# Hybrid decoder step with 32 experts: four rows of each gate-up matrix in one load of 4 MB, the other four in two loads of 2 MB

## What is computed

```python
x = x + (g_a * branch_a + g_b * branch_b) @ w_o           # mixer, from one projection h @ w_in
x = x + moe_ffn(rms_norm(x), ...)
# moe_ffn: 32 experts, the 4 best of a token's logits, their softmax as weights
hgu  = xblk @ w_gu[e] + b_gu[e]                            # 1024 x 2048, float32: 8 MB per expert
gate = minimum(hgu[:, :1024], 7); up = clip(hgu[:, 1024:], -7, 7)
act  = gate * sigmoid(1.702 * gate) * (up + 1)
y    = act @ w_down[e] + b_down[e]                         # 1024 x 1024, float32: 4 MB per expert
```

## Time and profile before

| what | us |
|---|---|
| median of three executions | 1143.05 |
| lowest and highest | 1141.73 and 1143.15 |
| the profiled execution's own time | 1143.05 |
| its span, from the first to the last instruction | 1141.3 |
| PE busy in the span | 1067.8 (94%) |
| mean rate of the DMA engines over the span | 380 GB/s |

### The profile page before, as it was taken

The page is one execution under the profiler, slowest core; times in us unless marked ns, Lnnn a source line. Parts: engine busy times, 40 slices in busy tenths (PEclk is TensorE's granted clock), DMA queues, the critical chain, the costliest instruction groups (busy, mean ns, idle before and its releaser), DMA issues.

```text
span 1141.3 us, 16947 instructions
## 1 busy us (share of the span) xinstructions
PE 1067.8 (94%) x6977; PEld 509.0 (45%) x6977; DVE 414.4 (36%) x716; ACT 173.0 (15%) x295; POOL 2.9 (0%) x12
## 2 busy tenths in 40 slices
PE   2999998699999999999999999999999999999995
PEld 2999964344433333333333434434333333333332
DVE  4366333523333333333333333333333333333344
ACT  4344112211111011011111111111111011001111
POOL 1000000000000000000000000000000000000000
PEclk9899999799999999999999999999999999999998
DMA  9464694799999999999999999999999999999993
GB/s 291 118 185 151 214 397 177 276 430 428 424 431 428 427 431 428 427 430 427 429 388 419 425 427 430 427 429 430 427 429 430 427 428 428 429 428 428 427 424 151
DMA packets 50997, 433.18 MB, mean 380 GB/s; under 512 B 5032, under 2 KB 21952, under 8 KB 25073
## 3 DMA queue, kind: packets, MB, share of 16 engines
q1 hardware_dynamic: 48535, 429.99, 90.9%
q10 hardware_dynamic: 2434, 2.79, 0.8%
HBM read 431.62 MB, written 1.39 MB: 379 GB/s over the span
## 4 chain that ended last, share of the span: by engine, by line
PE 56%; DMA 34%; DVE 4%; issue 3%; ACT 1%; SPq 1%; ACTq 0%; DVEq 0%
DMA down_ring<-in_w_down_dram 20%; PE PS L771 18%; PE PS L797 15%; DMA gu_ring<-in_w_gu_dram 14%; PE PS L627 9%; PE PS L736 3%; PE PS L748 2%; PE PS L679 2%; PE PS L663 1%; PE PS L660 1%; PE PS L749 1%; PE PS L784 1%; PE PS L782 1%; PE PS L811 1%; DVE pick_twice L1114 1%
## 5 line engine op out<-in xcount | busy, mean ns | idle before, releaser
L771 PE MATMUL PS<-gu_ring,XgT 128*64 128x512 f32 x2048 | 471.0, 599 | 9.3 <-DMA gu_ring<-in_w_gu_dram 8.6
L771 PEld LDWEIGHTS PS<-gu_ring,XgT 128*64 128x64 f32 x2048 | 134.3, 136 | 275.4 <-issue 242.3
L797 PE MATMUL PS<-down_ring,actT 128*64 128x512 f32 x992 | 221.7, 596 | 14.0 <-DMA down_ring<-in_w_down_dram 14.0
L1143 DVE TENSOR_TENSOR Y<-PS,Y 128x1024 f32<-128x1024 f32 (+1 forms) x96 | 117.0, 1220 | 267.9 <-PE PS L749 267.9
L1174 DVE SCALAR_TENSOR_TENSOR y_low<-PS,slot_gate,y_high 128x512 fp32r<-128x512 f32 x31 | 23.3, 751 | 310.8 <-ACT y_high L546 310.8
L797 PEld LDWEIGHTS PS<-down_ring,actT 128*64 128x64 f32 x992 | 67.7, 137 | 142.8 <-issue 118.7
L558 ACT ACTIVATE work<-PS 128x512 f32<-128x512 f32 x32 | 19.1, 597 | 471.5 <-PE PS L771 471.5
L627 PE MATMUL PS<-h_high,win_high 128*128 128x264 f32 (+1 forms) x256 | 75.1, 293 | 6.5 <-DVE h_low L930 6.5
L627 PE MATMUL PS<-h_high,win_low 128*128 128x264 f32 (+1 forms) x256 | 74.6, 291 | 0.0
L627 PE MATMUL PS<-h_low,win_high 128*128 128x264 f32 (+1 forms) x256 | 74.5, 291 | 0.0
L736 PE MATMUL PS<-pick,XP 128*128 128x64 bf16 x1792 | 58.6, 194 | 1.0 <-DVE pick L1106 1.0
(11 more groups left out here) (179 smaller groups left out, 659.8 us busy)
## 6 DMA issues: line engine op xcount, KB each, us to landing
gu_ring<-in_w_gu_dram SPq DMA_DIRECT2D x120, 2048.0 KB, 27.0
down_ring<-in_w_down_dram SPq DMA_DIRECT2D x62, 2048.0 KB, 23.1
gu_ring<-in_w_in_dram SPq DMA_DIRECT2D x16, 1024.0 KB, 5.5
gu_ring<-in_w_gu_dram SPq DMA_DIRECT2D x16, 1024.0 KB, 13.1
down_ring<-in_w_o_dram SPq DMA_DIRECT2D x1, 4096.0 KB, 17.4
gu_ring<-in_w_down_dram SPq DMA_DIRECT2D x4, 1024.0 KB, 25.7
gu_ring<-in_w_pool_up_dram SPq DMA_DIRECT2D x1, 2048.0 KB, 7.3
gu_ring<-in_w_conv_out_dram SPq DMA_DIRECT2D x1, 2048.0 KB, 7.5
```

The costliest lines, as they stand in the source:

```text
L771: last = mm(PS[SLOTS * h:SLOTS * h + SLOTS, b, :], XgT[:, k, :], w[:, D * b + HALF * h:D * b + HALF * h + HALF], start=(k == 0), stop=(k = ...
L797: last = mm(PS[SLOTS * h:SLOTS * h + SLOTS, bank, :], acts[:, f % 4, f // 4, :], weights[:, f, HALF * h:HALF * h + HALF], start=(f == 0), ...
L1143: tt(Y[rows, t, :].rearrange("p (h n) -> p h n", h=2), PS[rows, bank:bank + 2, :], Y[rows, t, :].rearrange("p (h n) -> p h n", h=2), ALU.a ...
```

## The change

`GROUPS` names the loads of a matrix by their first row and number of rows. Rows 0 to 3 come in one load of 4 MB, in which partition p takes four neighbouring rows of 512 in memory, 32 KB in one run. Rows 4, 5 and 6, 7 stay loads of 2 MB. Each matrix has three semaphores instead of four; the first stands at 16 times four after the single loads of items 0 and 1, which the wait's value takes in. SyncE waits ahead of the merged load for `gu_used` at 8i - 12, that is four rows of item i-2 instead of two. PE waits ahead of rows 0, 4 and 6. The gather takes its columns with a stride of four elements for rows 0 to 3, and `load_row` fetches its rows from the matching places.

```diff
+GROUPS = ((0, 4), (4, 2), (6, 2))
...
-        gu_landed = [sem(f"gu_landed{s}") for s in range(KT)]
+        gu_landed = [sem(f"gu_landed{s}") for s in range(2 * len(GROUPS))]
...
+        def group(k):
+            return next((g, at, n) for g, (at, n) in enumerate(GROUPS) if at <= k < at + n)
...
             def load_row(e, parity, k):
-                m, r = divmod(k, 2)
+                g, at, n = group(k)
                 sp.dma_start(gu_ring[:, KT * parity + k, :],
-                             w_gu[0, e, 2 * P * m:2 * P * m + 2 * P, :].rearrange("(p r) n -> p r n", r=2)[:, r, :]
-                             ).then_inc(gu_landed[CH * parity + m], 16)
-
-            def load_gu(e, parity, m):
-                src = w_gu[0, bass.ds(e, 1), 2 * P * m:2 * P * m + 2 * P, :].rearrange("a (p r) n -> (a p) (r n)", r=2)
-                sp.dma_start(gu_ring[:, KT * parity + 2 * m:KT * parity + 2 * m + 2, :].rearrange("p s n -> p (s n)"),
-                             src).then_inc(gu_landed[CH * parity + m], 16)
+                             w_gu[0, e, P * at:P * at + P * n, :].rearrange("(p r) n -> p r n", r=n)[:, k - at, :]
+                             ).then_inc(gu_landed[len(GROUPS) * parity + g], 16)
+
+            def load_gu(e, parity, g):
+                at, n = GROUPS[g]
+                src = w_gu[0, bass.ds(e, 1), P * at:P * at + P * n, :].rearrange("a (p r) n -> (a p) (r n)", r=n)
+                sp.dma_start(gu_ring[:, KT * parity + at:KT * parity + at + n, :].rearrange("p s n -> p (s n)"),
+                             src).then_inc(gu_landed[len(GROUPS) * parity + g], 16)
...
             def item_gu(i, e, parity):
-                for m in range(CH):
-                    sp.wait_ge(gu_used, 8 * i + (2 * m - 14))
-                    load_gu(e, parity, m)
+                for g, (at, n) in enumerate(GROUPS):
+                    sp.wait_ge(gu_used, 8 * i + (at + n - 16))
+                    load_gu(e, parity, g)
...
                 for k in range(KT):
-                    m, r = divmod(k, 2)
+                    _, at, width = group(k)
                     for n, (part, t) in enumerate(parts):
                         last = mm(PS[:, 5, SLOTS * k:SLOTS * k + SLOTS],
-                                  XP[:, part, 2 * P * m:2 * P * m + 2 * P].rearrange("t (p r) -> t r p", r=2)[:, r, :],
+                                  XP[:, part, P * at:P * at + P * width].rearrange("t (p r) -> t r p", r=width
+                                                                                   )[:, k - at, :],
...
                 for k in range(KT):
-                    if k % 2 == 0:
-                        pe.wait_ge(gu_landed[CH * u + k // 2], landed)
+                    g, at, width = group(k)
+                    if k == at:
+                        pe.wait_ge(gu_landed[len(GROUPS) * u + g], landed + 16 * (width - 2))
```

## The result

The changed kernel takes 1147.5 us (median of six executions, 1146.34 to 1148.81) against 1142.73 us. The ratio is 1.0045 with a 95% interval of 1.0033 to 1.0056, so 5.1 us slower with an interval of 3.8 to 6.4 (the difference of the two medians is 4.8). A second set of five executions gave 1.0045 again (1.0028 to 1.0062). The forecast was 1145.9 us, +2.8.

A forecast was written before the change was run, and what follows sets the result against it. The DMA stream was taken to bound two long stretches, so the end feels the stream's start, its rate and PE's work after the last awaited load. 1.4 - 2.0 + 3.4 = +2.8 us on 1143.05: 1145.9 us, range 1142.0 to 1149.5.

The forecast's parts named there:

- The bound: In two stretches, about 385 to 620 and 812 to 1003 us, DMA sets the pace; PE waits 1.95 us per item.
- One sign: Second DMA-bound stretch would begin one or two items sooner than 812 us.
- Term 2: Merged loads of items 2 to 28: longer runs save 0.075 us per load, -2.0 us in all.
- Term 3: Item 28, last gate-up wait: rows 0 to 3 become usable together, so PE lags two rows, +3.4 us.
- Term 1: Item 2's first gate-up load is issued at 223.69 instead of 220.26 into an empty queue: +1.4 us, at most 3.4.
- Small things: Gather's stride of four elements: taken as zero, at worst 0.45 us an item, 1.3 us behind the last wait.
- A: Merged loads: long runs bring nothing, cut up or cost by bytes; +4.8, 1147.9 us; chance 0.15.
- B: Not slower: merged loads gain more than the line, break-even 0.18 us per 4 MB; 1142.4 us at 0.2; chance 0.20.
- C: Long runs slower in memory: merged loads at 421 GB/s cost 0.16 us more each, 1152.2 us; chance 0.05.
- D: A fixed cost per queued load goes away, PE's DMA waits vanish, 29.4 us in all: 1113.7 us; chance 0.02.

The follow-up runs named there:

- SyncE's wait alone: Kernel before, with the first gate-up load of every item issued only when four rows are used: 1.0044, +5.0 us; repeated 1.0035, +4.0 us.
- the wait at item 2: Kernel before, with only the first gate-up load of item 2 waiting for four used rows instead of two: 1.0035, +4.0 us.
- the gather's stride: Kernel before, with the gather reading token columns at a stride of four elements for rows 0 to 3, weights in old order: 0.9997.
- the changed kernel with the old gather: Changed kernel, with the gather's old stride of two for all rows, weights in new order: 1.0040, +4.6 us against the kernel before.
- PE's wait alone: Kernel before, with PE waiting for rows 0 to 3 ahead of row 0, loads unchanged: 1.0028, +3.2 us.
- the first repair: Changed kernel, with item 2's rows 0 to 3 in two 2 MB loads, the first issued at two used rows: 1.0019, +2.2 us against the kernel before.
- the kernel with both waits: Kernel before, with first loads issued at four used rows and PE waiting for rows 0 to 3 ahead of row 0: 1.0067, +7.7 us.

## Why the prediction held, and where it was off

Direction and range were right; the forecast size, +2.8, was too small by 2.0 us against the medians and 2.3 against the ratio. By its steps:

**The bound.** There are still two stretches in which the DMA stream sets the pace and PE waits 1.6 to 1.9 us per item. Periods fell from 29.37 to 29.29 us (in the second stretch 29.2 and 29.4 in turn, of which the last two rows below show one), and items without waits took 27.50 us. One sign did not come: the second stretch did not begin an item or two sooner. In both kernels it begins with the same item, whose period is 27.95 us before and 28.97 now. Timeline of the changed kernel's first transposes:

```profile
703.30 0.55 PE L789 MATMUL PS<-ident,pick_twice 128*128 128x128 f32 x3
730.80 0.55 PE L789 MATMUL PS<-ident,pick_twice 128*128 128x128 f32 x3
...
902.56 0.55 PE L789 MATMUL PS<-ident,pick_twice 128*128 128x128 f32 x3
931.95 0.55 PE L789 MATMUL PS<-ident,pick_twice 128*128 128x128 f32 x3
```

**Term 2, the rate: right.** From the issue of the first gate-up load to the landing that PE waits for at item 27 (26 merged loads) the changed kernel takes 973.99 - 224.56 = 749.43 us and, in its second profile, 973.89 - 224.37 = 749.52. The kernel before takes, in its second profile, 970.58 - 219.12 = 751.46. That is 2.0 us, 0.077 per merged load, forecast 0.075. The other profiles agree: 751.3 to 751.6 us in four profiles without merged loads (both runs of SyncE's wait alone, the wait at item 2, the gather's stride) and 749.2 in the changed kernel with the old gather. The first profile of the kernel before has 974.12 - 220.26 = 753.86, as its load stood behind the 1 MB of the single row, 2.45 us. It can be read from single loads too: with the queue full a merged load lands 9.71 to 9.72 us behind the load ahead of it, two loads of 2 MB take 2 x 4.893 = 9.79. By the pages the changed kernel has 42124 DMA packets of 512 bytes or more and the kernel before 45965; the 3841 fewer are the 30 merged loads with 128 packets less each, so the longer runs were not cut up. The straight line through packets of 1 and 16 KB carries to 32 KB.

**Term 3, the lag behind the last wait: right.** It was forecast at +3.4 and measured alone at +3.2 (1.9 to 4.6). The waits went from three of 0.65 us to one per item, as written, and item 28 begins 3.8 us later than before where about 3.5 was expected.

**Term 1, the start of the stream: the mechanism right, the size wrong.** It was put at +1.4, with 3.4 as its most; alone it measured +4.0 (2.5 to 5.5). The step that failed is "the wait for that count now ends at 223.69": it took the time of four used rows, and the distance of the single row in front, from one execution. There item 0 began at full clock, two rows took 3.4 us, and the single row in front was issued 1.2 us before the load. In three further profiles of kernels with the old start (the second of before, PE's wait alone, the gather's stride) item 0 began at half clock and earlier; full clock at that place was seen once more, in the first repair's profile. In the second profile of before the single row, which waits for VectorE and not for PE, left 3.3 us ahead of the load (215.84 and 219.12). Two rows took 5.6 us there, and four took 9.4 in the profile of the wait at item 2 alone. The issue moved by 3.8 us and with nothing left in the queue nearly all of it was lost: the DMA share from 221 to 225 us is 0.94 in the second profile of before, 0.02 in the changed kernel and 0.05 with the wait at item 2 alone. The upper bound of 3.4 fell with the same assumption, since it was the full clock's time for two rows. No kernel with the late issue was profiled with the clock already full at item 0, so whether +1.4 would hold there is not shown. The merged load itself took 12.2 us from issue to landing in the first profile and 13.6 in the second, forecast 12.5.

With the measured 4.0 in place of 1.4 the sum is 4.0 - 2.0 + 3.4 = 5.4 us; measured 5.1, with an interval of 3.8 to 6.4.

**Small things.** The gather's price, taken as nothing with 1.3 us as its bound, is 0.12 us an item and vanishes in the total.

**Rivals.** A, long runs that bring nothing, would have given 1147.9 us, closer to the measured time than the forecast; yet its mechanism is refuted by the landings and periods, and the kernel with both waits speaks against it. A total that fits is no proof of its parts. B, which needs 0.18 us per merged load, and C, which makes them slower, are out with the 0.077. D, the fixed cost of about 2.0 us per load that the Trainium skill ("DMA: Bandwidth & Descriptors", the anatomy of one DMA) fits for loads issued by GpSimd, is not paid between the queued loads of SyncE here: a merger saved 0.08 us. It is seen where the queue is empty, as the cost of a new start: 2 MB took 7.6 us from issue to landing in the profile of the wait at item 2 alone, against 4.9 from landing to landing. (D's sum in the prediction is off by 0.1: 14 x 1.95 + 2 is 29.3.)

## What to carry to other kernels

A merged load is issued when the last of its space is free, and it is useful when the last of it has landed. Where a stream sets the pace, both delays cost nothing in its middle and their full length at its two ends, the first load and the last awaited one. Price the start from more than one execution, or from both levels of the clock: a count of used rows is a time only if PE's clock is known. The rate gain is per packet, so it is worth counting packets before merging: here 27 x 0.08 us stood against two delays of 3 to 4 us.

## What was not expected of the hardware

The granted clock fell to half for some 3 to 4 us at several places where PE was busy, and 24 matmuls then took 7.07 instead of 5.37 us. Windows of the changed kernel (granted clock third from the end):

```profile
850.00:970.00 120.00, 112.71 (x740) 46.13 (x736) 38.08 (x60) 12.27 (x24) 0.00 (x0) 1.00 1.00 429
...
976.00:980.00 4.00, 4.00 (x16) 1.51 (x14) 0.23 (x1) 0.00 (x0) 0.00 (x0) 0.76 1.02 434
1012.00:1016.00 4.00, 4.00 (x12) 1.24 (x14) 1.22 (x1) 0.00 (x0) 0.00 (x0) 0.57 1.01 430
```

Between 790 and 1003 us seven of the eight profiles of kernels with one undivided wait per item showed one to three such falls, the six profiles of kernels with three short waits none. They were largely absorbed by the next DMA wait: behind the fall at 943.46 in the profile of PE's wait alone it is 0.24 us instead of 1.9. Behind the last wait nothing absorbs the 1.7 us of a fall. There most profiles of either kind have one (seven of the eight, five of the six), such as the second profile of the kernel before:

```profile
1004.00:1008.00 4.00, 4.00 (x12) 1.12 (x12) 1.23 (x1) 0.00 (x0) 0.00 (x0) 0.73 1.01 430
```

So they don't explain the difference between the kernels. The first of these observations fits a wait of 1.6 to 1.9 us as a cause: the kernel with PE's wait alone differs from the one before in nothing but the waits. But no run varied the length of a wait step by step, and what sets the falls behind the last wait stays open.

The other surprise is the instruction transfers above: writing the last items out moves three pieces of 16 KB into the full stream, and one load in each of these two profiles lands 0.7 or 1.1 us late. That the one causes the other is not shown.
